# One-hot matrices of the expert gates: pairs of tokens innermost instead of sixteen

## What is computed

```python
i1 = jnp.take_along_axis(si[:, :, 0], ci // PEER_TOPK, axis=-1)
i2 = jnp.take_along_axis(si[:, :, 1], ci % PEER_TOPK, axis=-1)
eid = (i1 * N_KEYS + i2).reshape(t, PEER_HEADS * PEER_TOPK)
gate = jax.nn.softmax(cv, axis=-1).reshape(t, PEER_HEADS * PEER_TOPK)
act = jax.nn.gelu(jnp.einsum('td,ted->te', xb, u), approximate=False) * gate
return jnp.einsum('te,ted->td', act, vv)
```

## Time and profile before

| | |
|---|---|
| median of 3 runs | 6568.48 us (6561.36 to 6570.93) |
| profiled execution, own time | 6563.51 us |
| its span in the trace | 6561.7 us |
| mean granted TensorE clock | 0.866 of full speed |
| PE busy | 5080.0 us, 77% |
| DVE busy | 4664.0 us, 71% |
| ACT busy | 1674.3 us, 26% |
| gates stage, layer 0: first `hot` to issue of the last store | 1692.39 to 1884.02 us |

### The profile page before, as it was taken

One profiled execution on the slowest core, in us unless ns is written; L12 is line 12 of the kernel. 1 busy time (PEld: TensorE's weight loads), 2 busy tenths in 40 slices (PEclk: granted clock), 3 DMA queues, 4 the chain that ended last, 5 costly groups with the idle time before them and its releaser, 6 DMA issues. The chain is left out here.

```text
span 6561.7 us, 86274 instructions
## 1 busy us (share of the span) xinstructions
PE 5080.0 (77%) x28546; PEld 4493.4 (68%) x28546; DVE 4664.0 (71%) x8489; ACT 1674.3 (26%) x2238; POOL 1613.9 (25%) x1060
## 2 busy tenths in 40 slices
PE   7677776844689999988577777777753989998987
PEld 1366675744469998888567666666753578998886
DVE  0355555379759999999455555556389669999998
ACT  0122222211343333332221111112111433333332
POOL 0000000011026666665000000000011036666664
PEclk9788888877569999999789888888876579999998
DMA  7201110110159999998000000000110279999996
GB/s 269 86 30 36 36 36 7 52 36 22 77 225 369 363 367 352 348 350 312 28 24 24 23 24 24 20 19 29 40 36 14 103 284 368 367 368 347 346 352 245
DMA packets 397661, 1059.23 MB, mean 161 GB/s; under 512 B 36464, under 2 KB 143216, under 8 KB 390384
## 3 DMA queue, kind: packets, MB, share of 16 engines
q0 software_dynamic: 147456, 536.94, 22.1%
q1 hardware_dynamic: 249968, 519.27, 21.8%
HBM read 998.92 MB, written 57.15 MB: 161 GB/s over the span
## 5 line engine op out<-in xcount | busy, mean ns | idle before, releaser
L1995 POOL DMA_INDIRECT dense_rows<-in_peer_u_rows,dense_expert_ids x512 | 754.6, 1474 | 1017.0 <-DVEq L2011 587.9
L1604 POOL TENSOR_TENSOR top_w_lo<-top_w,top_w_hi 128x1024 fp32r<-128x1024 f32 x32 | 95.8, 3010 | 3418.5 <-ACTq L1572 3418.4
L1995 POOL DMA_INDIRECT dense_rows<-in_peer_v,dense_expert_ids x512 | 763.4, 1491 | 458.0 <-DVE sparse_acc L2051 349.8
L1905 PE MATMUL psum<-dense_a_hi,dense_v_hi 128*128 128x384 f32 x2048 | 704.2, 344 | 146.2 <-DVE residual L2038 143.6
L1890 PE MATMUL psum<-peer_in_hi,dense_u_hi 128*128 128x384 f32 x2048 | 697.8, 341 | 96.3 <-PE psum L1905 48.9
L1905 PE MATMUL psum<-dense_a_hi,dense_v_lo 128*128 128x384 f32 x2048 | 690.1, 337 | 0.0
L1905 PE MATMUL psum<-dense_a_lo,dense_v_hi 128*128 128x384 f32 x2048 | 689.8, 337 | 0.0
L1890 PE MATMUL psum<-peer_in_hi,dense_u_lo 128*128 128x384 f32 x2048 | 688.0, 336 | 0.0
L1890 PE MATMUL psum<-peer_in_lo,dense_u_hi 128*128 128x384 f32 x2048 | 687.6, 336 | 0.0
L2051 DVE SCALAR_TENSOR_TENSOR sparse_acc<-dense_rows,dense_weights,sparse_acc 128x1024 f32<-128x1024 f32 x512 | 656.0, 1281 | 37.1 <-DVE sparse_acc L2051 8.9
L2046 DVE CUSTOM_DVE_ANT_0 dense_rows<-dense_rows,sparse_in 128x1024 f32<-128x1024 f32 x512 | 604.5, 1216 | 0.0
(11 more groups left out here) (336 smaller groups left out, 10654.3 us busy)
## 6 DMA issues: line engine op xcount, KB each, us to landing
dense_u<-in_peer_u SPq DMA_DIRECT2D x256, 512.0 KB, 6.0
dense_v<-in_peer_v SPq DMA_DIRECT2D x512, 256.0 KB, 7.9
mod_w<-in_w_mod SPq DMA_DIRECT2D x24, 2048.0 KB, 7.7
gate_matrix<-gate_stage SPq DMA_DIRECT2D x12, 4096.0 KB, 11.1
dense_g<-gate_matrix SPq DMA_DIRECT2D x128, 384.0 KB, 7.8
gdn_w<-in_gdn_w_in SPq DMA_DIRECT2D x48, 512.0 KB, 3.3
ssd_w<-in_ssd_w_in SPq DMA_DIRECT2D x40, 512.0 KB, 3.3
top_w<-in_peer_w_q SPq DMA_DIRECT2D x32, 512.0 KB, 3.8
```

The lines of the kernel that those rows point to most:

```text
L1604: nc.gpsimd.tensor_tensor(wlo[:, s].rearrange("p k n -> p (k n)"), w[:, s].rearrange("p k n -> p (k n)"), whi[:, s].rearrange("p k n -> p ...
L1905: last = nc.tensor.matmul(ps[:, 2 + t, 0:ND], w[:, q % 4, cut], x[:, at], start=(e == 0 and m == 0), stop=(e == XB - 1 and m == 2))
L1995: pool.indirect_dma_start(out=rows[:, f % NBUF], out_offset=None, in_=table, in_offset=bass.IndirectOffsetOnAxis(ap=eid[:, c, p:p + 1], ax ...
```

## The change

The matrices' elements are laid out as (pair of tokens, key, token of the pair). A token's 128 elements are now 2 elements (4 bytes) apart. The number of elements, of instructions, of matmuls and of bytes stays the same. VectorE reads the picks as rows of 2 tokens, each read 128 times, where it read rows of 16.

```diff
-        iota = sb("iota", [P, NK, G], F16)
-        hot = sb("hot", [P, NK, G], F16)
-        second, high, low = (sb(n, [P, 2, NK, G], F16) for n in ("second", "high", "low"))
+        iota = sb("iota", [P, TG, NK, 2], F16)
+        hot = sb("hot", [P, TG, NK, 2], F16)
+        second, high, low = (sb(n, [P, 2, TG, NK, 2], F16) for n in ("second", "high", "low"))
...
-                                    nc.tensor.matmul(o, second[:, j, :, u], high[:, j, :, u], start=True, stop=False)
-                                    last = nc.tensor.matmul(o, second[:, j, :, u], low[:, j, :, u],
-                                                            start=False, stop=True)
+                                    at = (slice(None), j, u // 2, slice(None), u % 2)
+                                    nc.tensor.matmul(o, second[at], high[at], start=True, stop=False)
+                                    last = nc.tensor.matmul(o, second[at], low[at], start=False, stop=True)
...
-            nc.vector.tensor_copy(iota[:], bcast(k.c("iota"), 2, [P, NK, G]))
+            nc.vector.tensor_copy(iota[:], bcast(bcast(k.c("iota"), 1, [P, TG, NK]), 3, [P, TG, NK, 2]))
...
-                            kind = [bcast(now[:, m], 1, [P, NK, G]) for m in range(4)]
+                            kind = [bcast(now[:, m].rearrange("p (g o) -> p g o", o=2), 2, [P, TG, NK, 2])
+                                    for m in range(4)]
```

## The result

The changed kernel takes 6448.9 us (median of 4, 6446.77 to 6452.4) against 6566.97 us: a ratio of 0.9823, 95% interval 0.9811 to 0.9835. That is 118 us less; 6455 was forecast, in a range of 6440 to 6536. The spans of the two profiled executions differ by 6561.7 - 6446.3 = 115.4 us. In the gates stage the matmuls' two lines (L1710 and L1711) and those of VectorE's four operations (from L1759) are one higher than before; the lines between, such as L1727, are the same.

The account below looks back on a forecast made before the run. TensorE was taken to bound the gates stage at 7.69 us a unit, VectorE next at 5.37; saving 56.6 us a layer, 113 us for two, gave 6568.5 - 113 = 6455 us, range 6440 to 6536.

Parts of the forecast that it names:

- the order 7.69, 5.37, 4.5 us a unit: Gates stage before the change: time per unit of TensorE (7.69), VectorE if unheld (5.37) and ScalarE (about 4.5, estimated).
- The matmul's distance: Time between gate matmul starts: 0.240 us before, forecast between 0.107 and 0.148 us after, taken as 0.133.
- The argument that the weight load ends too early: Gate matmuls: the load, recorded with 0.148 us, ends over 0.09 us before the next matmul, so doesn't explain 0.240.
- Rival B: TensorE stays the bound, load and streaming in series: matmuls 0.217 us apart, 36 us saved, 6533 us; chance 0.13.
- VectorE's rate: VectorE's four f16 operations a unit were to stay at 1.226 us each, with rows of two picks.
- The other bound: VectorE's four operations at 2.29 us each if the double rate is lost, taken from nearby f32 operations.
- rival C: VectorE loses its double rate: 2.29 us an operation, 9.63 us a unit, 91 us slower, 6660 us; chance 0.11.
- The cast: Cast to `iota`, once a layer ahead of the loop: 1.226 us, taken as unchanged, at most 1.1 us more.
- The sum: Per layer, first `hot` to last matmul's end: 189.5 us before, 5.05 + 123.5 + 4.3 = 132.9 after, 56.6 saved.
- a last unit of 4.3 us on TensorE: Final term of each layer's forecast: TensorE finishing its last unit of matmuls at 0.133 us each, 4.3 us.
- PE's idle time: TensorE was to wait for VectorE in nearly every unit of the stage, about 1 us each.
- The explanation by lines of 16 bytes: Matmul operand reads: full speed needs two hits a line, so 2-byte types may step up to 8 elements free.

## Why the prediction was right

- **What bound the stage.** TensorE before, VectorE after. Both were read from the order 7.69, 5.37, 4.5 us a unit, and the added matmuls and the removed gaps show the second: what is added to TensorE costs almost nothing, and most of what is taken from VectorE comes back, until ScalarE binds. VectorE's unit was taken at 5.37 us and came at (1819.29 - 1696.02) / 23 = 5.36.
- **The matmul's distance.** The lower bound, 0.107 us, is what came; 0.133 was taken. The difference lies under VectorE, as was said. The argument that the weight load ends too early to be the cause held, but for 0.007 us (0.233 with only its layout mended). Rival B, 0.217 us, didn't come. Its answer, that the contiguous rows of 4-byte elements are limited by their loads, fits this but was tested by no run.
- **VectorE's rate.** 1.22 to 1.23 us, as taken. The other bound is real too: rows of one give 2.29 us, and the price worked out for rival C, 6660 us, met 6658. The Trainium skill's "Vector Engine (DVE) Microarchitecture Reference", section 5.1, has its limit exactly there (more than one element in the innermost dimension), and both runs agree with it.
- **The cast** stayed at 1.226 us, as taken.
- **The sum.** 56.6 us a layer forecast, 57.8 and 56.8 measured to the last copy's start; to the last store it was to be about 135 us and is 133.9 (issue at 1829.87). The medians differ by 118 us where 113 was forecast: 1.4 us of these 5 are the stage's (114.6 against 113.2), and the rest is inside the scatter of the runs, which the prediction put at 5 us.
- **A term with the wrong owner.** The sum ends with a last unit of 4.3 us on TensorE. It measured 3.6 us, and it is ScalarE's: TensorE starts all 32 matmuls of that unit within 1.8 us at the upper clock, and ScalarE's two copies in series end last. The size came out near by luck; it is one unit in 24, so little hung on it.
- **A step that was imprecise.** PE's idle time was put at about 1 us a unit. At 0.107 us a matmul it is 5.37 - 3.4 = 1.9 us, more where the clock rises; the waits give 2.3 us a unit.
- **A reason that was only half right.** The explanation by lines of 16 bytes, from the Trainium skill's "SBUF — State Buffer" (its note on cachelines), got the direction and the result for 2 tokens innermost. Its quantities did not hold: a step of 8 two-byte elements isn't free but costs 0.234 us a matmul, and two hits a line suffice only at the lower clock level, nearly (0.119 us against 0.107), and not at the upper (0.119 against 0.057). The measurement decides. The sum didn't rest on it.

## What to carry to other kernels

Look at the distance between matmul starts, not at their duration or at a PE that is 100% busy, and compare it with a contiguous matmul at the same granted clock: a distance 2.25 times too long was 57 us a layer. If a layout feeds two engines, ask what each needs in a row: here TensorE's moving operand of 2-byte elements wants several of them in 16 bytes (with four 0.057 us at the upper clock, with two 0.119), VectorE wants 2 adjacent ones, and a pair serves both. Then price the next engine in line from a stretch in which nothing holds it, for it, and not the speed-up of the first, gives the new time.

## What was not expected of the hardware

- **The moving operand's read has a time of its own.** Distance of the matmuls (us) by the steps of the two operands (bytes) and the granted clock; a dash where no stretch was read at that clock:

| kernel | moving | stationary | at 0.50 | at 1.00 |
|---|---|---|---|---|
| before | 32 | 32 | 0.240 | - |
| only stationary in pairs | 32 | 4 | 0.233 | - |
| eight tokens innermost | 16 | 16 | 0.234 | - |
| four tokens innermost | 8 | 8 | 0.119 | 0.119 |
| only moving in pairs | 4 | 32 | 0.107 | 0.065 |
| changed | 4 | 4 | 0.107 | 0.058 |
| one token innermost | 2 | 2 | 0.107 | - |

  The distance is the same at moving steps of 32 and 16 bytes and half of that at 8, as if each 16 bytes touched cost about 1.85 ns (an estimate: 0.233 / 128 = 1.82 and 0.119 / 64 = 1.86). At 4 bytes that would be 0.059 us, under the 0.107 of the lower clock and next to the 0.058 of the upper. That the clock plays no part in it is shown at the step of 8 bytes alone. What in the chip does so isn't shown by these runs.
- **A full PE at the lower clock, a half-idle one often at the upper.** Before, PE is busy 180 of 180 us at 0.50, and it is 170 of 170 at 0.50 with eight tokens innermost and with only the stationary operand in pairs. After, it is busy 57% and 55% of the two stretches of the stage, and the granted clock averages 0.71 and 0.75. With the extra matmuls it is 0.84 (81.94 us busy of the 120 from 1696 on). So a PE that is recorded as busy all through, with moving steps of 16 or 32 bytes, stayed at the lower level in all three kernels; why isn't shown. Here the higher clock was worth next to nothing, since VectorE set the pace and ScalarE the end.
